# A two-block transformer on one core: value projections with the activations stationary, split sums, and low and high weight matmuls in runs

## What is computed

```
h = rmsnorm(x, norm_attn[l])
(q_n, kc_n, vc_n, ks_n, vs_n, kw_n, vw_n, g_n, q_s, k_s, v_s,
 q_h, f_h, i_h, g_h, gates) = jnp.split(h @ w_in[l], split_at, axis=-1)
...
x = second_block(x, norm_w_2, w_in_2, ..., final_norm_w_2)
```

## Time and profile before

| | us |
|---|---|
| median of 3 runs | 2787.89 |
| profiled execution, its time | 2785.63 |
| profiled execution, its span | 2783.8 |
| TensorE matmuls busy | 2770.5 |
| TensorE weight loads busy | 2420.0 |
| VectorE busy | 1901.2 |
| ScalarE busy | 1269.3 |

### The profile page before, as it was taken

How to read it: one execution, slowest core, us unless ns; L and a number is a source line. 1 busy time by engine, 2 the same in 40 slices (tenths; PEclk the granted TensorE clock), 3 DMA queues, 4 the chain that set the end, 5 groups by cost and what they waited for, 6 DMA issues and landing times.

```text
span 2783.8 us, 41086 instructions
## 1 busy us (share of the span) xinstructions
PE 2770.5 (100%) x16216; PEld 2420.0 (87%) x16216; DVE 1901.2 (68%) x2128; ACT 1269.3 (46%) x1211; POOL 63.6 (2%) x113
## 2 busy tenths in 40 slices
PE   9999999999999999999999999999999999999998
PEld 8888888888888888888888888888888888888997
DVE  8676666677567879877777455765555766666686
ACT  6454457534545535444444333433334344443442
POOL 0000000000000000000000000000000000000100
PEclk9999999999999999999999999999999999999999
DMA  7664444565456555555555555555554466557763
GB/s 274 224 225 166 156 157 158 180 203 189 162 214 232 212 199 192 187 191 181 183 191 191 209 206 185 203 192 181 183 191 160 176 213 199 193 186 240 281 218 136
DMA packets 95726, 544.18 MB, mean 195 GB/s; under 512 B 11357, under 2 KB 25822, under 8 KB 35712
## 3 DMA queue, kind: packets, MB, share of 16 engines
q1 hardware_dynamic: 86384, 511.01, 52.3%
q0 software_dynamic: 9232, 31.57, 3.2%
HBM read 523.57 MB, written 23.04 MB: 196 GB/s over the span
## 4 chain that ended last, share of the span: by engine, by line
PE 99%; DVE 0%; DMA 0%; SPq 0%; ACT 0%; issue 0%; DVEq 0%
PE gemm L607 49%; PE gemm L610 25%; PE mix L607 11%; PE mix L610 6%; PE mix L602 1%; PE mix L601 1%; PE mix L600 1%; PE mix L718 1%; PE mix L913 1%; PE mix L1053 0%; PE mix L846 0%; PE mix L1082 0%; DMA raw<-wstream 0%; PE mix L764 0%; PE mix L1043 0%; DVE arena L2403 0%
## 5 line engine op out<-in xcount | busy, mean ns | idle before, releaser
L607 PE MATMUL gemm<-HX,whi 128*128 128x512 f32 x5440 | 1914.2, 399 | 0.0
L610 PE MATMUL gemm<-HX,wlo 128*128 128x256 f32 x5440 | 1469.2, 280 | 0.0
L1126 ACT ACTIVATE whi<-raw 128x2048 fp32r<-128x2048 f32 x466 | 891.5, 1914 | 1203.3 <-DMA raw<-wstream 1199.4
L1625 DVE TENSOR_TENSOR wlo<-raw,whi 128x2048 fp32r<-128x2048 f32 x465 | 1064.4, 2289 | 330.9 <-ACT whi L1126 329.6
L607 PEld LDWEIGHTS gemm<-HX,whi 128*128 128x128 f32 x5440 | 1005.9, 188 | 218.5 <-issue 0.9
L610 PEld LDWEIGHTS gemm<-HX,wlo 128*128 128x128 f32 x5440 | 1026.4, 189 | 28.8 <-issue 0.7
L1650 DVE TENSOR_REDUCE arena<-gemm 128x256 f32<-128x512 f32 (+1 forms) x157 | 108.2, 689 | 257.9 <-PE gemm L607 257.4
L607 PE MATMUL mix<-ACTX,whi 128*128 (+1 forms) x528 | 188.1, 395 | 0.0
L607 PE MATMUL mix<-UX,whi 128*128 128x512 f32 x416 | 146.6, 399 | 0.0
L610 PE MATMUL mix<-ACTX,wlo 128*128 (+1 forms) x528 | 146.1, 280 | 0.0
L607 PE MATMUL mix<-OX,whi 128*128 128x512 f32 x384 | 132.0, 398 | 0.0
(11 more groups left out here) (395 smaller groups left out, 2273.7 us busy)
## 6 DMA issues: line engine op xcount, KB each, us to landing
raw<-wstream SPq DMA_DIRECT2D x466, 1024.0 KB, 4.8
scratch<-gate_scratch POOLq DMA_DIRECT2D x12, 512.0 KB, 5.0
gate_scratch<-scratch SPq DMA_DIRECT2D x32, 128.0 KB, 4.6
GL<-gate_scratch POOLq DMA_DIRECT2D x8, 512.0 KB, 5.3
gate_scratch<-arena SPq DMA_DIRECT2D x32, 128.0 KB, 4.7
bias_scratch<-row_scratch POOLq DMA_DIRECT2D x21, 192.0 KB, 5.3
raw<-wstream SPq DMA_DIRECT2D x12, 256.0 KB, 7.6
btile<-bias_scratch POOLq DMA_DIRECT2D x21, 128.0 KB, 2.4
```

Of the source, the lines that this page charges most:

```text
L607: return pe.matmul(bank.rearrange("p (c t) -> p c t", c=2), whi[slot][:, w], mx, start=first, stop=last)
L610: return pe.matmul(bank[:, 0:T], wlo[slot][:, w], mh, start=False, stop=False)
L1126: f(whi[slot][:, :], raw[slot][:, :], ACT.Copy).then_inc(s["hi_ready"], 1)
L1625: tt(wlo[slot][:, :], raw[slot][:, :], whi[slot][:, :].bitcast(F32), ALU.subtract).then_inc(s["lo_ready"], 1)
```

## The change

Three things change.

1. *Value groups.* The blocks of value weights are taken in nine groups of four (`V_GROUPS`). In a group the activations are stationary and the weights move: for each half of the tokens and each slice of the contraction three matmuls of 512 columns (`values`) fill one bank with 128 tokens by 512 features. Each half has its own bank, and both are filled over all four blocks of the group. For this a block holds a quarter of each of four stream blocks, loaded in pieces of 2 KB per partition. VectorE copies each bank once (`tensor_copy`). The transposes and the copies after them are gone. For the recurrence ScalarE makes a copy of the second half of the activations with reversed tokens (`XV`, four copies of 128 x 1024). Group 0 takes places 16 to 19 of the stream, for which the two blocks before it change places with the next two.
2. *Split sums.* The squares are split like everything else: ScalarE writes their high part in fp32r (`nsa_hi`, `diag_hi`, `hg_hi`, `diff_hi`), VectorE the rest (`rest`), and the matmul with ones runs in fp32r, once for each part. Some of these steps move by one to four blocks.
3. *Order in a block.* `group` issues the first high matmul, then all low ones, then the remaining high ones, and, where only a part of the contraction is at hand, all high before all low, or the other way round. Only the very first block keeps its order.

```diff
+def group_of(n):
+    for g in V_GROUPS:
+        if g <= n < g + 4:
+            return g
+    return None
...
+            def group(bank, ks, total, w, mh, mx, slot):
...
+                ends = ks[-1] == total - 1
+                ahead = [k for k in ks if k == 0] if ends else ks
+                for k in ahead:
+                    ins = high(k)
+                for k in ks:
+                    ins = low(k)
+                for k in ks:
+                    if k not in ahead:
+                        ins = high(k)
+                return ins
...
-                    for k in range(KT):
-                        if fresh and k % fresh[2] == 0:
-                            pe.wait_ge(fresh[0], fresh[1] + k // fresh[2] + 1)
-                        ins = mm2(gps[bank][:, :], cols(k), mh(k), ml(k), slot, k == 0, k == KT - 1)
+                    for q in range(4 if fresh else 1):
+                        ks = range(4 * q, 4 * q + 4) if fresh else range(KT)
+                        if fresh:
+                            pe.wait_ge(fresh[0], fresh[1] + q + 1)
+                        ins = group(gps[bank][:, :], ks, KT, cols, mh, ml, slot)
...
+            def values(n, fresh=None):
...
+                for t in range(2):
+                    if b == 0:
+                        pe.wait_ge(s["evac_done"], u + t - 1)
+                    bank = gps[(u + t) % 2][:, :].rearrange("p (c f) -> p c f", c=4)
+                    for k in range(4):
+                        kk = 4 * b + k
+                        xh, xl = HH[:, kk, cols(t)], HL[:, kk, cols(t)]
+                        if t and B_HG < g < B_G:
+                            if k == 0:
+                                pe.wait_ge(s["xv"], b // 2 + 1)
+                            xh, xl = XV[kk // 8][0][:, kk % 8, :], XV[kk // 8][1][:, kk % 8, :]
+                        pe.matmul(bank, xh, wh[:, k], start=kk == 0, stop=False)
+                        pe.matmul(bank, xl, wh[:, k], start=False, stop=False)
+                        ins = pe.matmul(bank, xh, wl[:, k], start=False, stop=kk == KT - 1)
+                    if b == 3 and t == 0:
+                        ins.then_inc(s["v_half"], 1)
...
+            def sum_parts(bank, hi, lo):
+                pe.matmul(bank, ones_r[:, :], hi, start=True, stop=False)
+                return pe.matmul(bank, ones_r[:, :], lo, start=False, stop=True)
...
-                if b == 1:
-                    for i, v in enumerate((14, 15, 18, 19)):
-                        for t in range(2):
-                            ins = turn(M[:, 2 + i // 2, (i % 2) * T + t * P:(i % 2) * T + t * P + P], A[:, v, t * P:t * P + P])
-                    ins.then_inc(s["cmp_mm"], 1)
...
+            def rest(dst, src, hi, n):
+                dve.wait_ge(s["sum_hi"], n)
+                return tt(dst, src, hi.bitcast(F32), ALU.subtract)
```

More of the change, by code:

```diff
@@ L446, in reload, with reloads @@
                 load(n + RING, slot)
+            def reloads(a, b):
+                while a < b:
+                    n = 4 if group_of(a + RING) else plain_end(a + RING, b + RING) - RING - a
+                    n = min(n, b - a)
+                    blocks(sp, a, n, reload)
+                    a += n
             def spill(layer, first, u0):
@@ L736, in _ @@
             piece(2, 3)
[L737 to L740, removed]
+            for h in range(2):
+                pe.wait_ge(*half_done("lo", h))
+                ins = group(early_bank(0, 3), range(8 * h, 8 * h + 8), KT, cols, lambda k: UH[0][:, k, :], lambda k: ux(0, k), 3)
             ins.then_inc(s["gemm_done"], 1)
@@ L759, in _ @@
             pe.wait_ge(s["const_in"], 32)
-            advance(2)
+            advance(4)
             pe.wait_ge(s["head_sq"], 1)
             for b in range(6):
-                ins = pe.matmul(M[:, b, :], ones, SCR[:, b * 512:(b + 1) * 512], start=True, stop=True)
+                c = slice(b * 512, (b + 1) * 512)
+                ins = sum_parts(M[:, b, :], nsa_hi[:, c], SCRR[:, c])
             ins.then_inc(s["head_ss"], 1)
-            advance(N_SB1 - 3)
+            advance(N_SB1 - 5)
             pe.wait_ge(s["blk_l"], 2)
+            pe.wait_ge(s["head_rstd"], 1)
             for b in range(N_CW):
@@ L928, in _ @@
             for b in range(4):
-                ins = pe.matmul(M[:, b, :], ones, tiles(36 + 2 * b, 38 + 2 * b), start=True, stop=True)
+                c = slice(b * 512, (b + 1) * 512)
+                ins = sum_parts(M[:, b, :], hg_hi[:, c], hg_lo[:, c])
             ins.then_inc(s["head_ss"], 1)
@@ L968, in _ @@
                     for kk in range(2):
-                        ins = down(c, kk, kk, n0 % RING, first=kk == 0)
+                        down(c, kk, kk, n0 % RING, False, first=kk == 0)
+                for c in range(8):
+                    for kk in range(2):
+                        ins = down(c, kk, kk, n0 % RING, True)
                 ins.then_inc(s["gemm_done"], 1)
@@ L978, in _ @@
                         pe.wait_ge(s["f_lo"], FT)
-                    for kk in range(2):
-                        ins = down(c, kk, FT - 4 + 2 * b + kk, (n1 + b) % RING, last=b == 1 and kk == 1)
+                    for low in (True, False):
+                        for kk in range(2):
+                            ins = down(c, kk, FT - 4 + 2 * b + kk, (n1 + b) % RING, low, last=b == 1 and kk == 1)
                     if b == 0 and c == 7:
@@ L1074, in _ @@
                     for b in range(2):
-                        ins = pe.matmul(M[:, 4 + b, :], ones, SCR[:, b * 512:b * 512 + 512], start=True, stop=True)
+                        c = slice(b * 512, (b + 1) * 512)
+                        ins = sum_parts(M[:, 4 + b, :], diff_hi[:, c], SCRR[:, c])
                     ins.then_inc(s["head_ss"], 1)
@@ L1515, in _ @@
             advance(N_B + 1 - EARLY[2])
[L1516 to L1521 removed]
+            advance(2)
             act.wait_ge(s["fox_mm"], 1)
@@ L2028, in _ @@
                     me.link(ins)
-            advance(5)
+            advance(3)
+            rest(hg_lo[:, :], tiles(36, 44), hg_hi[:, :], 3).then_inc(s["head_sq"], 1)
+            advance(2)
             dve.wait_ge(s["hg_ge"], 1)
```

301 lines of the change are left out of this document (181 added, 120 removed).

## The result

The changed kernel takes **2753.22 us** (median of 4 runs, 2752.28 to 2753.88) against 2787.26 for the kernel before (4 runs, 2786.46 to 2788.72): ratio 0.9876, 95% interval 0.9861 to 0.9891, 34.0 us or 1.2% faster. The rival that comes nearest is B (2755): grouping pays.

What follows compares the result with a forecast made beforehand. TensorE was taken as the bound, busy 2770.5 of 2783.8 us. Terms -7.85 - 6.2 - 1.9 + 0 + 3.5 = -12.5 us gave 2773.1 profiled, 2775.4 by the median, forecast 2775; range 2754 to 2791.

Steps and rivals of the forecast that it cites:

- B: Rival for the new order in blocks: grouping pays, high and low run at pure-stream prices, -17.8 us, 2755 us; chance 0.26.
- Low together, high together: New order of 6576 steps in 411 blocks: taken as 0, with ends of +18.4 and -17.8 us.
- rival A: New order in blocks: grouping costs, runs keep the block seam's spacing, +18.4 us, 2796 us; chance 0.20 with milder forms.
- rival C: Weight matmuls: alternation hides the array's own pace, grouping frees 206 us, 2569 us; chance 0.01.
- Turned tiles: 72 transposes of value tiles leave TensorE at 0.109 us each: -7.85 us.
- Sums: Matmuls for the sums of squares in four places, split instead of float32, 0.235 for 0.429 us each: -6.2 us.
- Value groups: 36 value blocks with 24 matmuls of 512 columns and fewer weight loads, 5.60 us a block: -1.9 us.
- New waits: TensorE newly waiting for other engines in three places: +3.5 us, with 0 and 9 as ends.
- (a): Near the third compression block: VectorE's scaling by the norm delays its split, TensorE waits 2.5 us.
- (b): Before the third sum: TensorE waits for VectorE's rest of 2048 columns, 0.5 us.
- (c): Value groups fill both banks and need the previous evacuation earlier: 0.5 us, ahead of the second model block's first group.
- rival D: The two banks: each of nine value groups waits about 1 us for a late evacuation, +8.5 us, 2784 us; chance 0.08.

Runs made afterwards that it cites:

- e1: The changed kernel with high and low matmuls alternating again in every block, the rest of the change kept: 2773.93 us, ratio 0.9947 to the kernel before.
- e2: The kernel before with only the new order inside its blocks, nothing else changed: 2763.84 us, ratio 0.9914.
- e7: The changed kernel with eight further orders of 512- and 256-column matmuls in the feed-forward projection, eight blocks each: 2762.87 us, one execution.
- e5: The changed kernel with six forms of block in the feed-forward projection (other low matmuls, widths or orders), ten blocks each: 2790.36 us, one execution.

## Why the prediction was wrong

**The step that failed is "Low together, high together", set at 0.** Measured, it is -20.7 us in the changed kernel (e1; -19.7 with the chips' difference) and -24.4 alone (e2). Everything else together was forecast at -12.5 and is -14.3 (e1). The working failed in two places.

First, the fit. I took alternation as the neutral case and got the price of a load from it: three lows in 360 ns against a step in 353.2. But the 353.2 held a surcharge of 6.7 ns for the change of length. Without it a step is 346.7, and the fixed cost of a matmul 13.3 ns, not 6.8. "The fit by columns and loads gives exactly 0" was circular: it was made from the alternation that it was to judge.

Second, the ends. I took 0.235 (the seam) and 0.2305 (narrow weights) as the two ends of a high, with 0 in the middle because the ends lay evenly. Neither is the steady spacing. e7 shows what the seam was: highs just behind a low. The argument "against" rival A, that a seam is a moment, was right; the one against B, the narrow weights, was wrong, for full weights run faster (0.2267). B was the mechanism with the right sign, and even its highs at 0.2305 were above the 0.2287 measured in runs of sixteen. That its total, 2755, comes within 2 us is partly luck: it had -17.8 for the order and -4.4 for the value groups where the runs show -20.7 and about -5.9, and 3.5 us of new waits where there are 5.7.

Two figures of the working are off by a rounding that decides nothing: (3.85 - 0.39) / 15 is 0.2307, not 0.2305, and rival C's 325 ns a step would be 28.2 ns less, 185 us and not 187.

Why then not 411 x 0.086 = 35 us? Because not every block was slow before. A stretch of the kernel **before**, behind a run of transposes:

```profile
574.99 0.27 PE L610 MATMUL gemm<-HX,wlo 128*128 128x256 f32 x1
...
575.34 0.28 PE L610 MATMUL gemm<-HX,wlo 128*128 128x256 f32 x1
...
575.69 0.27 PE L610 MATMUL gemm<-HX,wlo 128*128 128x256 f32 x1
...
576.03 0.28 PE L610 MATMUL gemm<-HX,wlo 128*128 128x256 f32 x1
```

Lows start 1.04 / 3 = 0.347 us apart: here alternation runs without surcharge (high to low 231 ns, low to high 116). The kernel before has 376 undivided blocks at L607 and L610 outside the branches and `down`. 105 of them stand behind small work, and 66 of these ran so; their median was 5.64 us, with a first high that costs 0.314 us. In the changed kernel most such blocks take 5.64 to 5.67, so they gained nothing by the median. Of the 271 behind another block 37 ran so; the median of all 271 is 5.653, and 5.567 after the change. Most telling is the second half of `down`. Ten of its blocks, first of the kernel before, then of the changed one:

```profile
1660.83:1716.29 55.46, 55.46 (x322) 1.00 0.54 195
...
1641.08:1696.74 55.66, 55.66 (x322) 1.00 0.52 189
```

There the old order took 5.547 us a block, the law's time without any surplus, and the grouped one takes 5.567: where alternation is in its fast rhythm, grouping costs 0.02 us. (In e1 the same half alternates at 5.65, so the place alone does not decide.) Over all alternating steps of the kernel before about a quarter ran at 347 ns. I had read one window in a long loop and taken it for all 6576 steps. What sets which of the two rhythms alternation takes wasn't tried, so it stays open whether the gain could be had without grouping.

**The other terms.**

- *Turned tiles*: -7.85 forecast; the 72 rows of 0.109 us are gone.
- *Sums*: as forecast, 0.236 against 0.429.
- *Value groups*: 5.44 us a block where I had 5.60, by the same wrong fit. From start to start the 36 blocks take 200.6 us, 3.0 of it above 5.44 in three that hold a wait; 36 x 5.653 is 203.5, so they gain about 5.9 without the waits if all had run at 5.653 before, where I had 1.9 and a bound of 4.4. The Trainium skill's rule (page "TensorE: Matmul & The Clock Gate", section "Part 2: What happens when you issue a matmul"), that loading weights takes no read bandwidth from a running matmul, gave 0 as I read it. By the law of e5 eight load-and-matmul pairs fewer at equal columns save 107 ns of a block, and the rest of the 0.21 us is the surplus of alternation; whether the load or the matmul's start has that price, no run tells apart.
- *New waits*: 5.7 us for the 3.5 forecast. Of (a)'s 2.5 us 1.0 came where it was forecast; 1.1 more came ahead of the scaling, where I had nothing. (b) is 0.3 of 0.5. (c) is 1.2 us at the first group of the second block of the model where I had 0.5, since all that VectorE has to do ahead of it is in a row; and one more group waits 0.4 us, so rival D is true for two groups of nine. The rest is many small waits of TensorE that comes earlier everywhere.

Re-measured, the terms give -7.85 - 6.2 - 5.9 + 5.7 = -14.25 beside e1's -14.3. That they meet so closely is partly luck: e1's interval reaches from 11 to 19, its own waits are 7.5 us and not 8.3, and a wait costs more than its row shows (1.20 us at 1802.48, but 1.59 - 0.23 from start to start).

## What to carry to other kernels

Where matmuls of different length alternate, read their price from streams of one length as well, and never fit a price of columns and loads from the mixture that the change takes apart. Here 512 columns cost 226.7 and 256 cost 120.0 ns, so one run of sixteen in place of the slow alternation was worth 1.5% of a block, and fewer, longer matmuls (24 for 32) another 2%. A window in a loop stands for the loop: count the blocks that run otherwise before you multiply. Where alternation already runs at the price of the pure streams, grouping has nothing to give. And where small blocks follow each other, look whether the loads keep up before moving another engine's work.

## What was not expected of the hardware

- 13.3 ns on top of 0.417 ns a column for every matmul with new weights, worked out from 256 and 512 columns (e5 and the long runs).
- A surplus in the highs behind a low, up to 20 ns net over five of them, that depends neither on the tensor nor on the half of the bank, but comes with the change of length (e5, e7).
- Alternation has two steady rhythms in the kernel before, 347 and 353.3 ns a step, and keeps the one that it has over whole blocks, 5.547 us each in the second half of `down` and 5.653 in most others.
- Runs of four are no better than runs of two (5.600 and 5.594 us); the full gain came with a run of sixteen (5.567), and nothing between was tried in whole blocks.
